# Lacing the two late layers: differential attention beside three products, output-projection chunks beside attention units

## The chip, the cores and the metric

One core of one Trainium2 chip runs the whole program; the other cores are idle. The metric is the device time of one execution in microseconds (us). Three executions of the kernel before gave 1477.77, 1477.8 and 1483.44 us, median 1477.8. Engines are named PE (TensorE), DVE (VectorE), ACT (ScalarE), POOL (GpSimd) and SP (SyncE, which issues the weight loads). Each engine runs its own instructions strictly in program order and waits on semaphores for the others.

## What is computed

A first block (gated linear attention, block attention, attention to a memory, then a mixture of 32 experts) gives `x`, 256 tokens by 1024 in float32. The second block, where the change lies, has two layers:

```
def second_block(x, c, ada_w, ada_b, ...):
    cond = jax.nn.silu(c)
    for l in range(2):
        mod = cond @ ada_w[l] + ada_b[l]                    # 1024 x 6144
        sh1, sc1, g1, sh2, sc2, g2 = split(mod, 6)
        h = rms_norm(x, norm_mix[l]) * (1 + sc1) + sh1
        y = even_mixer(h) if l == 0 else odd_mixer(h)
        x = x + g1 * (y @ w_out[l])
        h = rms_norm(x, norm_ffn[l]) * (1 + sc2) + sh2
        x = x + g2 * ((silu(h @ wg) * (h @ wu)) @ wd)       # hidden 2816

def even_mixer(h):      # aq, ak, av, bq, bk, bv, iq, ik, iw = columns of h @ w_in
    aq, ak = rms_norm per 64-wide head            # 4 heads x 2 maps
    ya = rms_norm(softmax(aq1 ak1') v - lam * softmax(aq2 ak2') v)
    score = sum over 8 heads of relu(iq ik') * iw;  sel = top 64 keys of each query
    yb = softmax over sel of rms_norm(bq) rms_norm(bk)'  times bv     # 8 heads
    return concat(ya, yb)

def odd_mixer(h):       # 16 query heads, 4 key heads, window of 128, a sink logit per head
```

## The kernel before

**Loads.** Weights come in loads of up to 2 MB on SP's DMA queue, in one fixed order, into a ring of `NR = 5` slots. `make_plan` writes that order out by hand. A load waits (`sp.wait_ge(*freed[before[k]])`) until the last user of what lay in its slot is done, and every later load stands behind that wait.

**Chunks.** A product (`ak`, `aq`, `av`, `kvi`, `tli`, `bq` in layer 0; `kvo`, `q0`, `q1` in layer 1), an output projection (`wo`) or a feed-forward matrix is worked in chunks of a 128-row strip. For each chunk ACT makes the rounded part (`W_c_r` or `X_c_r`), DVE the rest (`ring_r`), and PE multiplies in three terms: 12 matmuls of 512 columns, or 24 of 256. `Feed` has PE some chunks behind the two others (`lag`, 5 in the products).

**Modulation.** The 24 strips v0 to v23 of `cond @ ada_w` (`ada`) are spread between other work. A *run* needs a load of its own of 2 MB and is 8 matmuls on PE, `ps7<-ring,csr`; ACT copies the sum out; a *close*, 4 matmuls `ps7<-ones,acc`, spreads it, and DVE writes it to `modc`. All use bank 7, so the next run waits for DVE's `modc` of the strip before. The trace counts two passes for each f32 matmul: 16 records a run, 8 a close. `plan.rows` says at which chunk ("f"), norm ("n") or attention unit ("u") each stands.

**Attention.** `attend(n)` works units of a head and a query half in a pipeline of ticks: PE in each tick turns the weights of unit t-3, makes the two scores of unit t, multiplies the values of unit t-4; DVE takes maxima and makes weights, ACT exponentials. t2 (differential, 8 units), t3 (selected, 8) and t4 (sliding window, 16) are run one after another with nothing but modulation runs and side work (headnorms, turns, the indexer's selection) between them. Two units' scores are on different banks (`2 * (U % 2) + m`).

**Order.** Layer 0: `ak aq av kvi tli bq`, then t2 with the indexer beside it, t3, `wo1`, feed-forward. Layer 1: `kvo q0 q1`, t4, `wo2`, feed-forward. Only the first two chunks of `wo` are begun (split) inside the attention before them.

Of the kernel before, what the change touches and what calls it, by code (L numbers as in the profile page):

```python
# [76 lines left out]
class Feed:  # L77
# [36 lines left out]
def pipeline(n, *stages):  # L114
    for t in range(n + max(lag for lag, _ in stages)):
        for lag, stage in stages:
            if 0 <= t - lag < n:
                stage(t - lag)


class Plan:
# [51 lines left out]
    def ffn(self, l, turn_run, run):  # L173
# [63 lines left out]
def build(nc, A, out_ap, dbg):  # L237
    ctx = ExitStack()
    with ctx:
# [175 lines left out]
        beside = {first["wo", j] + c for j in range(3) for c in range(2)}  # L415
        buf, last_use, previous = [], {}, []
        for i in range(nch):
            if i == first["ak"]:
                last_use = {}
            b = min(range(3 if i in beside else 6), key=lambda z: (last_use.get(z, -1), z))  # L420
# [135 lines left out]
        bank = (0, 0, 1, 1, 2, 2, 3, 4)  # L556
        block_of = lambda f: ps[bank[f]][:, half(f) if f < 6 else slice(0, 256)]
# [14 lines left out]
        class Attn:  # L572
            total, values, outs, done = 0, [], 0, 0

            def __init__(self, X, hL, units):
# [3 lines left out]
                self.pv, self.fin, self.oh = [], [], []  # L579
                for unit in units:  # L580
# [207 lines left out]
        def scalar(act):  # L788
# [59 lines left out]
            def attend(n, beside, chunks=(), XF=None):  # L848
# [21 lines left out]
                def copies(u):  # L870
# [4 lines left out]
                    copy(at_n.pT[:, U % 2, 0:w], ps[4 + U % 2][:, 0:w], up=s_cp)  # L875
# [7 lines left out]
                pipeline(len(at_n.units), (4, copies), (5, fins), (1, weights), (0, scores), (4, ahead))  # L883

            def out_proj(j, tb, XF, attended):
                if j < 2:
                    act.wait_ge(s_gc, j + 1)
                    for c in range(4):
                        act.wait_ge(s_tp, tb + c + 1)
                        copy(hH[:, c, :], ps[4 + c][:, 0:256], scale=gc, up=s_tH)  # L890
                act.wait_ge(s_fin, attended)
                for c in range(2, 8):
                    begin(first["wo", j] + c, XF)
# [160 lines left out]

            def work_av():
# [27 lines left out]
            feed.product(first["av"], 4, ends("av", av, [4, 5], work_av()))  # L1083
            feed.product(first["kvi"], 4, ends("kvi", kvi, [0, 1], headnorm(heads(kvp[:, :, 0:64]), 1)))
            feed.product(first["tli"], 2, ends("tli", tli, [2, 3], steps(3)))
            feed.product(first["bq"], 4, ends("bq", bq, [4, 5], work_bq()))
            feed.drain()
            side.until(ev, "qk")
            attend(2, 2)
# [7 lines left out]
            attend(3, 2, [first["wo", 1], first["wo", 1] + 1], XFc)  # L1097
            side.end()
            ada(("o", 1))
            out_proj(1, 28, XFc, t3.end)  # L1100
# [65 lines left out]
        def vector(dve):  # L1166
# [88 lines left out]
            def attend(n, beside, chunks=(), XF=None):  # L1255
# [13 lines left out]
                def weights(u):  # L1269
# [7 lines left out]
                    for m in range(2):  # L1277
                        V(dve.tensor_tensor_reduce, at_n.pb[:, k, 257 * m:257 * m + nk], ps[2 * (U % 2) + m][:, 0:nk], unit.bias,
# [25 lines left out]
                pipeline(len(at_n.units), (1, weights), (2, norms), (5, fins), (0, scores), (4, ahead))  # L1304

            def out_proj(j, gain, hL, XF):
                if gain:
                    V(ts, gc, gain[0], gain[1], None, ALU.mult, up=s_gc)
                    for c in range(4):
                        dve.wait_ge(*C.next(s_tH))  # L1310
                        V(stt, out=hL[:, c, :], in0=ps[4 + c][:, 0:256], scalar=gc, in1=hH[:, c, :].bitcast(FP), op0=ALU.mult,
                          op1=ALU.subtract, up=s_tL)
                for c in range(2, 8):
                    begin(first["wo", j] + c, XF)
# [22 lines left out]
            def add_xT(gate, n, end):  # L1337
                for f in range(8):
                    if f == 7:
                        dve.wait_ge(s_use, end)  # L1340
                    elif f % 2 == 0:
                        dve.wait_ge(s_f, 4 * n + f // 2 + 1)
                    V(stt, out=xT[:, f, :], in0=block_of(f), scalar=gate[:, f:f + 1], in1=xT[:, f, :], op0=ALU.mult,
# [295 lines left out]

            def work_av():  # L1640
# [62 lines left out]
            feed.product(first["av"], 4, ends(work_av()))  # L1703
            feed.product(first["kvi"], 4, ends(work_kvi()))
            feed.product(first["tli"], 2, ends(work_tli()))
            feed.product(first["bq"], 4, ends(work_bq()))
            feed.drain()
            side.until(ev, "qk")
            attend(2, 2)
# [87 lines left out]
        def tensor(pe):  # L1797
# [108 lines left out]
            def features(i, j, last, xH, xL, XF):  # L1906
# [5 lines left out]
                for f in range(8):  # L1912
                    for n, row in both_last:
                        w, wl, wh = chunk(n, 1, XF)
                        for m, (x_, z) in enumerate(((xH, wh), (xL, wh), (xH, wl))):
                            t = mm(block_of(f), z[:, 0, 128 * f:128 * f + 128], x_[:, row, :],
                                   j == 0 and m == 0 and (f % 2 == 0 or f == 7), j == last and n == i and m == 2 and f % 2 == 1)
                        if f == 7:
                            t.then_inc(s_use, 1)
                    if j == last and f in (1, 3, 5, 6):  # L1920
                        t.then_inc(s_f, 1)
                if j == last:
                    for f in range(8):
                        free[bank[f]] = C.next(s_xd)
# [610 lines left out]
```

## Time and profile before

| | us |
|---|---|
| three runs, median | 1477.8 |
| profiled execution: time / span | 1480.7 / 1478.7 |
| PE busy | 1207.3 (82%) |
| DVE busy | 615.7 (42%) |
| ACT busy | 476.1 (32%) |
| DMA queue q1 | 367.26 MB, 64.7% of 16 engines |
| first block, until PE starts the second | about 697 |

Busy shares are of the whole span. In the profile PEclk is the TensorE clock granted, as a share of full speed; "PE idle, <- X" says whose result ended an idle stretch.

### The profile page before, as it was taken

How to read it: one execution, taken by the hardware profiler on the slowest of the kernel's cores; microseconds unless marked ns; L12 is line 12 of the kernel's file. 1: busy time of each engine (PE TensorE's matmuls, PEld its weight loads, DVE VectorE, ACT ScalarE, POOL GpSimd, SP SyncE). 2: the span in 40 equal slices, each digit the busy share in tenths (PEclk: the TensorE clock that was granted, in tenths of full speed). 3: DMA queues.
4: the chain of work that ended last, by engine and by line, in shares of the span. 5: the costliest groups of instructions: out<-in, count | busy, mean ns of one | idle time of the engine just before them, and what ended most of it. 6: DMA issues, size and time to landing. Idle time of an engine off the chain costs nothing.

```text
span 1478.7 us, 19441 instructions
## 1 busy us (share of the span) xinstructions
PE 1207.3 (82%) x7691; PEld 883.7 (60%) x7691; DVE 615.7 (42%) x1239; ACT 476.1 (32%) x769; POOL 7.6 (1%) x54
## 2 busy tenths in 40 slices
PE   5878886775676756847897888999999978999998
PEld 4655464442333323413675337899898734999986
DVE  3472643110010000101753576655535756565553
ACT  4561530100000000002532335554433447465441
POOL 1000000000000000000000000000000000000000
PEclk9897788888888877977897668899999988999999
DMA  8442347999999999999536431865536462665520
GB/s 292 172 152 76 115 173 320 428 430 429 430 430 428 430 430 428 430 425 403 197 129 228 171 114 58 253 207 201 195 145 226 171 253 90 203 196 174 203 109 29
DMA packets 121728, 368.67 MB, mean 249 GB/s; under 512 B 9842, under 2 KB 56093, under 8 KB 110878
## 3 DMA queue, kind: packets, MB, share of 16 engines
q1 hardware_dynamic: 120556, 367.26, 64.7%
q8 instruction: 64, 1.05, 0.3%
q10 hardware_dynamic: 1074, 0.08, 0.1%
q14 instruction: 34, 0.28, 0.1%
HBM read 366.28 MB, written 1.05 MB: 248 GB/s over the span
## 4 chain that ended last, share of the span: by engine, by line
PE 61%; DMA 21%; DVE 9%; ACT 5%; issue 3%; SPq 1%; DVEq 0%; ACTq 0%
PE ps L1810 58%; DMA more<-in_w_down_dram 7%; DMA more<-in_w_gate_dram 7%; DMA more<-in_w_up_dram 6%; PE ps L1814 3%; DVE st L32 2%; DVE ring_r L32 2%; DVE R_c L32 1%; SPq L664 1%; DVE R_a L32 1%; DVE X_c L32 1%; ACT X_c L32 1%; DVE sc L32 1%; ACT R_a L32 1%; ACT hn L32 1%
## 5 line engine op out<-in xcount | busy, mean ns | idle before, releaser
L1810 PE MATMUL ps<-hT_r,ring_r 128*128 128x256 f32 x864 | 245.5, 284 | 0.0
L1810 PE MATMUL ps<-ring,xg 128*32 128x512 f32 x640 | 140.4, 725 | 121.5 <-DMA more<-in_w_gate_dram 42.6
L1810 PEld LDWEIGHTS ps<-hT_r,ring_r 128*128 128x128 f32 x864 | 167.8, 194 | 0.0
L1810 PEld LDWEIGHTS ps<-ring,xg 128*32 128x32 f32 x640 | 35.2, 131 | 217.2 <-issue 217.2
L32 DVE TENSOR_TENSOR ring_r<-ring,W_c_r 128x1024 fp32r<-128x1024 f32 x94 | 115.2, 1226 | 97.5 <-ACT W_c_r L32 94.1
L1810 PE MATMUL ps<-R_c_r,W_c_r 128*128 128x256 f32 x608 | 153.1, 284 | 0.0
L32 DVE TENSOR_TENSOR ring_r<-ring,X_c_r 128x1024 fp32r<-128x1024 f32 x88 | 107.8, 1225 | 98.4 <-ACT X_c_r L32 95.7
L1810 PE MATMUL ps<-R_c_r,X_c_r 128*128 128x256 f32 x576 | 148.2, 285 | 0.0
L32 ACT ACTIVATE W_c_r<-ring 128x1024 fp32r<-128x1024 f32 x94 | 99.7, 1060 | 89.2 <-PE ps L1810 84.5
L32 ACT ACTIVATE X_c_r<-ring 128x1024 fp32r<-128x1024 f32 x88 | 93.3, 1061 | 90.3 <-PE ps L1810 85.4
L1810 PE MATMUL ps<-hT_r,W_c_r 128*128 128x256 f32 x416 | 119.0, 286 | 1.9 <-DVE R_c_r L32 1.8
L1810 PE MATMUL ps<-hT_r,X_c_r 128*128 128x256 f32 x416 | 119.0, 286 | 1.8 <-DVE R_c_r L32 1.8
L32 DVE TENSOR_TENSOR x<-x,ps 128x512 f32<-128x512 f32 x36 | 24.8, 688 | 228.9 <-PE ps L1810 228.6
L1810 PEld LDWEIGHTS ps<-R_c_r,W_c_r 128*128 128x128 f32 x608 | 109.2, 191 | 0.0
L1810 PEld LDWEIGHTS ps<-R_c_r,X_c_r 128*128 128x128 f32 x576 | 104.6, 192 | 1.7 <-issue 1.7
L1810 PE MATMUL ps<-ring_r,hT_r 128*128 128x512 f32 (+1 forms) x240 | 97.7, 407 | 0.0
L1810 PEld LDWEIGHTS ps<-hT_r,W_c_r 128*128 128x128 f32 x416 | 79.9, 192 | 2.7 <-DVE R_c_r L32 2.2
L1810 PEld LDWEIGHTS ps<-hT_r,X_c_r 128*128 128x128 f32 x416 | 79.9, 192 | 2.6 <-issue 2.5
L1810 PE MATMUL ps<-ring,csr 128*32 128x512 f32 x384 | 66.8, 830 | 13.0 <-DVE modc L32 12.5
L1810 PE MATMUL ps<-more,xg 128*32 128x512 f32 x384 | 72.6, 747 | 0.0
L1810 PE MATMUL ps<-sel,hn 128*128 128x128 f32 x256 | 63.1, 408 | 2.4 <-DVE sel L32 2.4
L1810 PEld LDWEIGHTS ps<-sel,hn 128*128 128x128 f32 x256 | 61.8, 336 | 3.2 <-DVE flag L32 2.5
(281 smaller groups left out, 1874.5 us busy)
## 6 DMA issues: line engine op xcount, KB each, us to landing
ring<-in_ada_w_dram SPq DMA_DIRECT2D x24, 2048.0 KB, 8.2
ring<-in_w_gate_dram SPq DMA_DIRECT2D x20, 2048.0 KB, 15.9
ring<-in_w_up_dram SPq DMA_DIRECT2D x20, 2048.0 KB, 20.7
ring<-in_w_down_dram SPq DMA_DIRECT2D x20, 2048.0 KB, 16.4
more<-in_w_up_dram SPq DMA_DIRECT2D x12, 2048.0 KB, 24.4
more<-in_w_gate_dram SPq DMA_DIRECT2D x12, 2048.0 KB, 23.1
more<-in_w_down_dram SPq DMA_DIRECT2D x12, 2048.0 KB, 23.6
ring<-in_ffn_gate_dram SPq DMA_DIRECT2D x22, 1024.0 KB, 5.6
```

What stands on the lines that cost most here:

```text
L32: op(*args, **kw).then_inc(sem, 1)
L664: sp.dma_start(dst, src).then_inc(s_w[slot[k]], 16)
L1810: return pe.matmul(out, lhsT, rhs, start=start, stop=stop, skip_group_check=True)
L1814: return pe.transpose(out, in_, ident[0:n, 0:n])
```

## The change

Three things, all in the second block.

1. `attend` now returns its ticks as a generator. `beside_first` steps t2's ticks between the chunks of `kvi`, `tli`, `bq`, with `lag` 2; these three products all write banks 4 and 5. Their ACT and DVE buffers are taken from 3 instead of 6 (`narrow`). Since t2 now starts before `kvi`'s second chunk, the turn of `aq` must be done by then, and PE, DVE and ACT run `side.until(ev, "qk")` there.
2. `beside` steps t3's and t4's ticks with a chunk of `wo1` or `wo2` every second tick (from tick 2, from tick 4); these sums are on banks 3, 4, 5, 7. For t3, modulated heads from t2 are turned in tick 5 (`mix_turned`).
3. To free banks, scores of t2, t3, t4 are on banks 0 and 1 for every unit, and turned weights on 2 (t2: 2 and 3). Bank 7 is needed for `wo`, so fewer modulation strips lie in the attentions, and more in the products and feed-forwards.

```diff
+def beside(g, units, feed, i0, start, hook):
+    n = 0
+    for t in range(units + 5):
+        next(g, None)
+        if t == start + 3:
+            feed.side.end()
+            hook()
+        if t >= start and (t - start) % 2 == 0:
+            if n < 8:
+                feed(i0 + n)
+                n += 1
+            else:
+                feed.one()
+    for k in range(n, 8):
+        feed(i0 + k)
+    feed.drain()
...
-    for name in ("aq", "av", "kvi"):
-        p.product(name, 4)
+    for name in ("aq", "av"):
+        k = p.load("w", name)
+        p.first[name] = len(p.chunks)
+        for q in range(4):
+            if q == 1:
+                p.ada(("f", len(p.chunks)))
+            if q == 3:
+                p.close(("f", len(p.chunks)))
+            p.feed(k, q)
+    p.product("kvi", 4)
     p.product("tli", 2)
-    p.ada(("f", len(p.chunks)))
     p.product("bq", 4)
-    p.close(("f", len(p.chunks) - 1))
     p.units(2, 8, (0, 2, 4, 6))
-    p.units(3, 8, (0, 2, 4, 6), 2, 1)
-    p.close(("o", 1))
+    p.units(3, 8, (0, 2), 0, 1)
     p.out_proj(1)
-    p.ffn(0, True, 6)
+    p.ffn(0, True, (6, 12))
...
     p.product("q0", 4)
-    p.product("q1", 4)
-    p.units(4, 16, (0, 2, 4, 6, 8, 10, 12), 8, 2)
-    p.close(("o", 2))
+    p.ada(("f", len(p.chunks)))
+    k = p.load("w", "q1")
+    p.first["q1"] = len(p.chunks)
+    for q in range(4):
+        if q == 2:
+            p.close(("f", len(p.chunks)))
+        if q == 3:
+            p.ada(("f", len(p.chunks)))
+        p.feed(k, q)
+    p.units(4, 16, (1, 3, 5), 1, 2)
     p.out_proj(2)
-    p.ffn(1, False, None)
+    p.ffn(1, False, (6, 12))
...
+        for t_ in (t2, t3, t4):
+            t_.score = lambda U, m: m
+        t2.turned = lambda U: 2 + U % 2
+        t3.turned = t4.turned = lambda U: 2
...
+        def beside_first(feed, g, ready):
+            feed.lag = 2
+            for i in range(first["kvi"], first["bq"] + 4):
+                feed(i)
+                if i == first["kvi"]:
+                    ready()
+                else:
+                    next(g)
+            feed.drain()
+            run(g)
```

**What moves, place 1.** PE between the second block's first modulation run (v4) and the first chunk of `ak` (`ps0<-W_c_r,hT_r`). Before:

```order
L1810 MATMUL ps7<-ring,csr 32x512 [waits s_w3,s_gather_out]
L1810 MATMUL ps7<-ring,csr 32x512 x7
L1810 MATMUL ps6<-ident,sc 128x128 [waits s_norm_rstd_spread]
L1810 MATMUL ps6<-ident,sc 128x128
L1810 MATMUL ps0<-W_c_r,hT_r 128x512 [waits s_lo,s_tL,s_moe_hid,s_moe_silu]
```

After:

```order
L1857 MATMUL ps7<-ring,csr 32x512 [waits s_w3,s_gather_out]
L1857 MATMUL ps7<-ring,csr 32x512 x7
L1857 MATMUL ps6<-ident,sc 128x128 [waits s_norm_rstd_spread]
L1857 MATMUL ps6<-ident,sc 128x128
L1857 MATMUL ps7<-ones,acc 128x1 [waits s_ada_copied]
L1857 MATMUL ps7<-ones,acc 128x1 x3
L1857 MATMUL ps7<-ring,csr 32x512 [waits s_w0,s_ada_col]
L1857 MATMUL ps7<-ring,csr 32x512 x7
L1857 MATMUL ps0<-W_c_r,hT_r 128x512 [waits s_lo,s_tL,s_moe_hid,s_moe_silu]
```

The close of v4 and the run of v5 now stand ahead of the first chunk. `s_w0` is v5's load; `s_ada_col` is DVE's write of `modc` for v4. On DVE that write stands here, after:

```order
L32 SCALAR_TENSOR_TENSOR R_c_r<-R_c,modc,hT_r 128x256 [waits s_tL,s_tH]
L32 TENSOR_TENSOR ring_r<-ring,X_c_r 128x1024 [waits s_tL,s_hi]
L32 TENSOR_TENSOR ring_r<-ring,X_c_r 128x1024 [waits s_lo,s_hi]
L32 TENSOR_TENSOR modc<-ps7,cols 128x4 [waits s_lo,s_ld1,s_ada_closed]
L32 TENSOR_TENSOR ring_r<-ring,W_c_r 128x1024 [waits s_ada_col,s_hi]
```

It is behind the last modulated rest (`R_c_r`) and two splits of later chunks.

**Place 2.** PE at the end of `ak` (`ps1`) and the start of `aq` (`ps2`). Before, one product follows the other:

```order
L1810 MATMUL ps1<-X_c_r,hT_r 128x512
L1810 MATMUL ps1<-X_c_r,R_c_r 128x512
L1810 MATMUL ps1<-ring_r,hT_r 128x512
L1810 MATMUL ps2<-X_c_r,hT_r 128x512 [waits s_lo,s_moe_y,s_scatter_added]
```

After, v6's run is between them:

```order
L1857 MATMUL ps1<-X_c_r,hT_r 128x512
L1857 MATMUL ps1<-X_c_r,R_c_r 128x512
L1857 MATMUL ps1<-ring_r,hT_r 128x512
L1857 MATMUL ps7<-ring,csr 32x512 [waits s_w2,s_ada_col]
L1857 MATMUL ps7<-ring,csr 32x512 x7
L1857 MATMUL ps2<-X_c_r,hT_r 128x512 [waits s_lo,s_moe_y,s_scatter_added]
```

Slot 2 (`s_w2`) held `ak`'s weights, so v6's load is issued only when the row above the run is done. The planner's table of slots gives the same for v7 (slot of `av`), v9 (slot of `kvi`), v10 (slot of `tli`) and v18 (slot of `kvo`).

**Place 3.** PE after the last chunk of `kvi`. Before, the close of v5 and `tli` (on `ps2`, `ps3`) follow:

```order
L1810 MATMUL ps1<-X_c_r,hT_r 128x512
L1810 MATMUL ps1<-X_c_r,R_c_r 128x512
L1810 MATMUL ps1<-ring_r,hT_r 128x512
L1810 MATMUL ps7<-ones,acc 128x1 [waits s_ada_copied]
L1810 MATMUL ps7<-ones,acc 128x1 x3
L1810 MATMUL ps2<-X_c_r,hT_r 128x256 [waits s_lo,s_evacuated]
```

After, a tick of t2 and v9's run are between `kvi` (`ps5`) and `tli` (`ps4`):

```order
L1857 MATMUL ps5<-W_c_r,hT_r 128x512
L1857 MATMUL ps5<-W_c_r,R_c_r 128x512
L1857 MATMUL ps5<-ring_r,hT_r 128x512
L1861 MATMUL ps3<-ident,X_c 128x128 [waits s_attn_normed,s_evacuated]
L1861 MATMUL ps3<-ident,X_c 128x128
L1857 MATMUL ps0<-R_c 128x128 [waits s_attn_max]
L1857 MATMUL ps1<-R_c 128x128 [waits s_attn_max]
L1857 MATMUL ps7<-ring,csr 32x512 [waits s_w3,s_ada_col]
L1857 MATMUL ps7<-ring,csr 32x512 x7
L1857 MATMUL ps6<-R_c,X_c 128x128 [waits s_attn_copied,s_head_copied]
L1857 MATMUL ps4<-W_c_r,hT_r 128x256 [waits s_lo,s_evacuated]
```

What moved in: turned weights on `ps3`, the two scores on `ps0` and `ps1`, a run that waits for slot 3 (`kvi`'s own, just freed), and a value product on `ps6`.

## Rows read from the trace of the kernel before

**Rows 1.** Windows: stretch, length, busy PE, PEld, DVE, ACT, POOL, clock, DMA share, GB/s

```profile
700.00:792.00 92.00, 83.43 (x387) 64.70 (x386) 51.59 (x101) 35.44 (x47) 0.00 (x0) 0.89 0.53 186
792.00:858.00 66.00, 48.20 (x208) 26.26 (x208) 36.44 (x137) 21.44 (x57) 0.69 (x2) 0.66 0.45 160
858.00:900.00 42.00, 32.61 (x200) 16.04 (x200) 30.88 (x104) 19.41 (x54) 0.00 (x0) 0.70 0.30 101
925.00:1145.00 220.00, 212.86 (x1732) 204.22 (x1731) 117.77 (x155) 98.80 (x126) 0.00 (x0) 0.94 0.61 206
1184.00:1275.00 91.00, 77.77 (x563) 50.26 (x562) 53.77 (x158) 50.21 (x115) 0.00 (x0) 0.87 0.47 162
```

**Rows 2.** PE's waits, 740 to 950: us in total, times, longest

```profile
PE ps L1814 <- DVE R_c L32: 7.7, 5, 5.0
PE ps L1810 <- DVE modc L32: 6.3, 5, 2.2
```

**Rows 3.** PE's timeline, 709 to 715: start, length, instruction

```profile
709.71 0.47 PE L1810 MATMUL ps<-W_c_r,hT_r 128*128 128x512 f32 x1 [1.77 <-DVE R_c_r L32]
...
710.53 0.63 PE L1810 MATMUL ps<-W_c_r,hT_r 128*128 128x512 f32 x1
710.95 0.63 PE L1810 MATMUL ps<-W_c_r,R_c_r 128*128 128x512 f32 x1
...
714.60 0.39 PE L1810 MATMUL ps<-ring_r,hT_r 128*128 128x512 f32 x1
714.83 0.40 PE L1810 MATMUL ps<-W_c_r,hT_r 128*128 128x512 f32 x1
```

**Rows 4.** DVE's timeline, 720 to 724

```profile
720.69 2.56 DVE L32 TENSOR_TENSOR ring_r<-ring,X_c_r 128x1024 fp32r<-128x1024 f32 x2 [1.24 <-ACT X_c_r L32]
```

**Rows 5.** PE's timeline, 755 to 760

```profile
755.48 1.05 PE L1810 MATMUL ps<-ones,acc 128*128 128x1 f32 x8 [1.66 <-DVE R_c L32]
757.11 2.61 PE L1810 MATMUL ps<-ring,csr 128*32 128x512 f32 x16 [0.57 <-DVE modc L32]
```

**Rows 6.** DMA issues of the page: KB each, median us from issue to landing

```profile
ring<-in_ada_w_dram SPq DMA_DIRECT2D x24, 2048.0 KB, 8.2
```

**Rows 7.** Groups by form, 792 to 858: count, busy, mean ns, idle before

```profile
L1810 PE MATMUL ps<-R_c,X_c 128*128 128x128 f32 x24 | 6.9, 418 | 4.6 <-DVE hn L32 4.6
L1814 PE MATMUL ps<-ident,X_c 128*128 128x128 f32 x12 | 3.5, 358 | 0.0
L32 DVE CUSTOM_DVE_ANT_0 X_c<-ps,negd 128x256 f32<-128x256 f32 x8 | 3.4, 424 | 0.8 <-DVE modc L32 0.7
L32 DVE COPY hn<-ps 128x128 f32<-128x128 f32 x8 | 2.3, 291 | 4.6 <-PE ps L1810 4.2
```

**Rows 8.** PE's timeline, first instruction of `wo1` and the one behind it

```profile
902.09 0.55 PE L1810 MATMUL ps<-hT_r,W_c_r 128*128 128x256 f32 x1
...
926.09 4.28 PE L1810 MATMUL ps<-ones,sc 128*128 128x1 f32 x32
```

**Rows 9.** PE's timeline, 1066 to 1075, in the feed-forward of layer 0

```profile
1066.71 0.95 PE L1810 MATMUL ps<-ones,acc 128*128 128x1 f32 x8
1071.26 3.64 PE L1810 MATMUL ps<-ring,csr 128*32 128x512 f32 x16 [3.60 <-DVE modc L32]
```

**Rows 10.** PE's timeline in t4 and `wo2`: units 2, 4, 6, first and last of `wo2`

```profile
1200.38 0.80 PE L1810 MATMUL ps<-R_c 64*128 64x128 f32 x4
...
1207.53 0.49 PE L1810 MATMUL ps<-R_c 64*128 64x128 f32 x4
1207.95 1.92 PE L1810 MATMUL ps<-ring,csr 128*32 128x512 f32 x16
...
1213.33 0.49 PE L1810 MATMUL ps<-R_c 64*128 64x128 f32 x4
...
1251.70 0.58 PE L1810 MATMUL ps<-hT_r,W_c_r 128*128 128x256 f32 x1 [1.84 <-DVE R_c_r L32]
...
1276.60 3.63 PE L1810 MATMUL ps<-ones,sc 128*128 128x1 f32 x32
```

More of the change, by code:

```diff
@@ L411, in build @@
         nch = plan.end
-        beside = {first["wo", j] + c for j in range(3) for c in range(2)}
+        narrow = {first["wo", j] + c for j in range(3) for c in range(8 if j else 2)}
+        narrow |= set(range(first["kvi"], first["bq"] + 4))
         buf, last_use, previous = [], {}, []
@@ L881, in fins, with mix_turned @@
                         copy(hH[:, unit.dst, unit.out], ps[6][:, unit.out], up=s_oh)
[L883 to L893, printed above, removed]
+                return ticks(len(at_n.units), (4, copies), (5, fins), (1, weights), (0, scores), (4, ahead))
+            def mix_turned(j, tb):
+                act.wait_ge(s_gc, j + 1)
+                for c in range(4):
+                    act.wait_ge(s_tp, tb + c + 1)
+                    copy(hH[:, c, :], ps[mixed[j][c]][:, 0:256], scale=gc, up=s_tH)
             def modulated(l, which, n, ready, hooks={}):
@@ L1082, in scalar @@
             feed.product(first["aq"], 4, ends("aq", aq, [2, 3], work_aq()))
[L1083 to L1089, printed above, removed]
+            feed.product(first["av"], 4, ends("av", av, [4, 5], steps(2)))
+            feed.then[first["kvi"] + 3] = ends("kvi", kvi, [4, 5], headnorm(heads(kvp[:, :, 0:64]), 1))
+            feed.then[first["tli"] + 1] = ends("tli", tli, [4, 5], steps(3))
+            feed.then[first["bq"] + 3] = ends("bq", bq, [4, 5], work_bq())
+            beside_first(feed, attend(2, 2), lambda: side.until(ev, "qk"))
             def work_sub():
@@ L1302, in fins, with mix_turned @@
                           up=s_fin)
[L1304 to L1314, printed above, removed]
+                return ticks(len(at_n.units), (1, weights), (2, norms), (5, fins), (0, scores), (4, ahead))
+            def mix_turned(j, gain, hL):
+                V(ts, gc, gain[0], gain[1], None, ALU.mult, up=s_gc)
+                for c in range(4):
+                    dve.wait_ge(*C.next(s_tH))
+                    V(stt, out=hL[:, c, :], in0=ps[mixed[j][c]][:, 0:256], scalar=gc, in1=hH[:, c, :].bitcast(FP), op0=ALU.mult,
+                      op1=ALU.subtract, up=s_tL)
             def add_x(gate, n, end):
@@ L1702, in vector @@
             feed.product(first["aq"], 4, ends(work_aq()))
[L1703 to L1709, printed above, removed]
+            feed.product(first["av"], 4, ends(steps(2)))
+            feed.then[first["kvi"] + 3] = ends(work_kvi())
+            feed.then[first["tli"] + 1] = ends(work_tli())
+            feed.then[first["bq"] + 3] = ends(work_bq())
+            beside_first(feed, attend(2, 2), lambda: side.until(ev, "qk"))
             def work_sub():
@@ L2154, in tensor @@
             pe.wait_ge(s_fin, t1.end)
-            out_proj(0, hL_ma, XF, 16)
+            mix_turned(0)
+            feed = out_proj(0, hL_ma, XF, 16)
+            for c in range(8):
+                feed(first["wo", 0] + c)
+            feed.drain()
             pe.wait_ge(s_hn0, 3)
```

152 lines of the change are left out of this document (77 added, 75 removed).

## Prediction

> **What bounds the kernel now.** I read first the windows by stage, then PE's waits, then PE's timeline stage by stage. In the second block PE sets the end. In the feed-forward, 925 to 1145, it is busy 212.86 of 220 us; in the products before t2, 83.43 of 92 (8.6 us idle). Only the attentions have room: 48.20 of 66 us with t2 and the indexer, 32.61 of 42 with t3, 77.77 of 91 with t4 and `wo2` [rows 1]. There DVE (36.44 and 30.88 us) is no bound by itself either; units wait for each other in a chain of PE, DVE and ACT, and PE is granted only 0.66 and 0.70 of its clock. In PE's list of waits from 740 to 950 the longest entries name DVE: headnorm results (`R_c`, 7.7 us, one of 5.0) and `modc`, 6.3 [rows 2]. There is no row for a DMA: every load lands before its user. So the change can win the idle time of the attentions, about 18 + 9 + 13 us and the slow clock in them, if it adds no waits of its own elsewhere. I find that it does, by its placing of the modulation strips.
>
> **Layer 0, until `bq` is done.** In before that is T = 791.9, the start of t2. Five terms.
>
> (a) v5's run now stands ahead of `ak`. Before, the first chunk begins at 709.71 [rows 3]. Now PE must wait there for v4's `modc`, which DVE writes behind all modulated rests and two splits; these two end at 720.69 + 2.56 = 723.25 [rows 4], and what they need doesn't come from `ak`. Write and run: 723.25 + 0.2 + 3.64 (a run after a wait, rows 9) = 727.1. The first chunk starts at 727.1 instead of 709.71: **+17.4**. ACT and DVE have their next chunks split by then, but only six buffers are there, and PE is the bound behind it, so nothing of it is won back.
>
> (b) More strips. Before, this stretch held two closes and a run, 1.05 + 2.61 + 0.95 = 4.6 [rows 5, 9]. Now the runs of v6 to v10 and six closes. Four of the runs follow a wait for a load and take 3.64, one 1.92 [rows 9, 10]; closes 1.05: 14.6 + 1.9 + 6.3 = 22.8. **+18.2.**
>
> (c) t2's own PE work now lies in it: all value products are 6.9 us and turns 3.5 [rows 7], scores some 0.6 for each of 8 units [rows 10]: 15.2 for all in the slow clock. With most units in and a faster clock beside chunks I take **+10** (8 to 15).
>
> (d) PE's waits. A load takes 8.2 us from issue to landing [rows 6]. v6's load needs `ak`'s slot, and v6's run is the very next thing on PE: 8.1. v7 after `av`: only a unit's scores between, 7.5. v9 after `kvi`: a turn and scores, 7.2. v10 after `tli`: a headturn besides and what DVE is late, 5.0. Sum 27.8. The turn of `aq` must be ready by `kvi`'s second chunk, where before all of `av` lay between; the nearest row is the wait of 5.0 for a headnorm [rows 2], and two splits of 1.28 [rows 4] stand before it on DVE: 7.4. Together 35.2, less the 8.6 that were there [rows 1]: **+27**. Bounds: from 15 (if two of the waits fall into one of DVE's) to 36.
>
> (e) Behind a long wait, a chunk's first nine matmuls come 0.42 us apart instead of 0.23 [rows 3], 1.7 us a time; three times: **+5**. This is the TensorE clock at its lower level (1.2 of 2.4 GHz): after PE's idle 3.60 us the run took 3.64, in the flow 1.92 [rows 9, 10]. The Trainium skill (TensorE: Matmul & The Clock Gate, HAM oscillation — how this bites in real kernels) describes just this: bursts of matmuls parted by waits for a DMA start in the slow clock each time. By that rule the sum stays as it is, and without it it would be 5 us less and (b) 7 less; the trace agrees.
>
> Sum 17.4 + 18.2 + 10 + 27 + 5 = **+78**.
>
> **Layer 0, from there to the end of `wo1`.** Before, 791.9 to 926.1 [rows 8], 134.2 us. Now t2's work on DVE is gone from it: the wide maxima 3.4 and the copies of `hn` 2.3 [rows 7], and with the narrow maxima, weights, norms and small steps about 18 of the 36.44 [rows 1]. The indexer's chain (relu, weighted sums, eight rounds of maxima, then t3) stays and has to wait for `bq`'s and `tli`'s results as before. Of `wo1`, 24.0 us for 8 chunks [rows 8], half is in t3 now (chunk c ≥ 4 waits for the last unit): −12. Together −30, with a little single banking **−29** (−18 to −37). Where it could be less: a chunk's two splits cost DVE 1.28 and ACT alike inside ticks that the chain fills.
>
> **Feed-forward 0**: one run and close more, no stall: 1.92 + 0.95 = **+2.9**.
>
> **Layer 1.** In `q1` the close of v16 and run of v17 meet the stall seen at 1066.71 (0.95, then 3.60 idle and a run of 3.64 [rows 9]): +8.2. Then close v17 1.05, wait for v18's load (slot of `kvo`, issued long before) at most 1.5, run 1.92: **+12.7** (5 to 15; in before a like stall lies in unit 0, and I leave units 0 and 1 as they were, since v18's close and v19's run will stand there). From unit 2 to the end of `wo2`: before 1276.60 − 1200.38 = 76.2 [rows 10]. Pairs of units with a run and a close take 5.8 (1207.53 to 1213.33 [rows 10]), so without these 2.8. After: three pairs with strips, 16.5; then a pair and a chunk of 2.9 are 5.7, and with both scores on the same two banks for each unit, so that a unit's scores wait for the maxima of the one before, I take 6.4, four times: 25.6; the tail 10.6; what is left of `wo2` 7.5. Sum 60, −16; against it stands that each pair could as well wait for DVE (splits and weights), 1 us each. **−14** (−20 to −6). Feed-forward 1 gets v22 and v23, the wide gates: 1.92 + 2.25 each, **+8.3**. Layer 1: **+7**.
>
> **Sum.** 78 − 29 + 2.9 + 7 = +59. The profiled execution took 1480.7, so 1539.6; it was 2.9 above the median of the three, so **1537**.
>
> **The rivals.**
>
> 1. *Loads and restarts cost little* (chance 0.12). PE's waits in (d) replace others, since DVE and ACT are behind there too and catch up. For it: DVE's and ACT's splits of the next chunk do run on during a wait. Against: before has only 8.6 us to be replaced [rows 1]. Time: without 27 + 5, and 7 less in (b): 1498.
>
> 2. *Laced ticks are slower than I make them* (0.12). With three chunk buffers and lag 2, each tick of t2 beside a chunk goes through DVE's queue: split, maxima, weights; with one pair of score banks unit t+1 can't start before the maxima of t. Every tick of 10, 6 and 8 would be 1 to 2 us longer, at 24 ticks +25 to +40: 1562 to 1575. Against: DVE is busy only 36.44 of 66 us [rows 1].
>
> 3. *It wins, because PE's idle time is filled* (faster, 0.04). Mechanism: strips' loads land behind other work, v5's run costs only itself, and attention lies under chunks. Then (a), (d) and (e) fall away, 17.4 + 27 + 5 + 7: 1481, and layer 0's second half and t4 at their best bounds (−8, −6) give 1467. It decides at PE's wait before v6: if PE isn't seen idle for a DMA there, this or rival 1 holds; if the first chunk of `ak` begins near 711 as well, this. Beside it: the Trainium skill (Perfetto Trace Analysis, Optimization Strategy) says that interleaving stretches with different busiest engines may help. This case's stretches are such [rows 1]; the rule speaks for the change, and says nothing of loads that come in a ring.
>
> **How the numbers follow.** My own case has 0.70; its range, from the bounds of (c), (d), the second half, t4 and q-phase taken together as roots (2 to 5, 12, 11, 8, 8: about ±18), is 1519 to 1556. Rival 1 gives 1498 and rival 2 1562 to 1575; with 0.12 each, the range for 8 in 10 takes in part of both: 1506 to 1563. 0.02 are left for no change by other sums. About 0.5%, 7 us, is what a measurement can tell: faster 0.04, same 0.03, slower 0.93.
>
> **What the profile after would show.** PE idle about 12 us before the first `ak` chunk, with `modc` as its releaser; PE idle for `ring<-in_ada_w_dram` about 8, 7.5, 7 and 5 us behind `ak`, `av`, `kvi` and `tli`; runs of 3.6 us behind these; the stretch from the end of `bq` to `wo1`'s end some 105 us; t4 from unit 2 to the end of `wo2` about 62; the feed-forwards as before but for three strips. I would be wrong most likely in the ticks beside chunks, where no row of before shows a product and an attention sharing DVE.

## The result

The changed kernel takes 1564.0 us (median of 4 runs, 1563.0 to 1566.7), the kernel before 1479.6 beside it: ratio 1.057, 95% interval 1.0542 to 1.0598. It is slower by about 84 us, as forecast in sign, but 1 us above my range and 27 above my value. The profiled span is 1562.6 us against 1478.7.

The windows of the changed kernel, by the same stretches as [rows 1] (length, busy PE, PEld, DVE, ACT, POOL, clock, DMA share, GB/s):

```profile
702.00:794.00 92.00, 58.05 (x258) 41.13 (x257) 36.83 (x74) 25.08 (x34) 0.00 (x0) 0.76 0.36 129
794.00:873.00 79.00, 57.82 (x304) 38.49 (x304) 29.92 (x96) 24.82 (x56) 0.00 (x0) 0.82 0.24 87
873.00:985.00 112.00, 74.61 (x410) 52.81 (x409) 67.89 (x190) 38.86 (x83) 0.69 (x2) 0.70 0.37 132
985.00:1203.00 218.00, 211.33 (x1743) 201.97 (x1742) 117.42 (x155) 99.14 (x128) 0.00 (x0) 0.98 0.61 208
1256.00:1350.00 94.00, 73.02 (x492) 51.62 (x492) 54.19 (x157) 47.55 (x110) 0.00 (x0) 0.82 0.28 92
```

In the first 92 us of the second block PE is now busy 58.05 us, where it was busy 83.43 [rows 1]. The feed-forward is as it was. Where the time went, by PE's start times (us) at the same places of the two profiles:

| place on PE | before | after | added here | my term |
|---|---|---|---|---|
| start of the second block | 696.93 | 698.73 | 1.8 | 0 |
| first chunk of `ak` | 709.71 | 729.09 | 17.6 | 17.4 |
| `bq` done | 791.9 | 872.7 | 61.4 | 60 |
| `wo1` done | 926.09 | 984.69 | −22.2 | −29 |
| first chunk of `kvo` | 1144.76 | 1203.41 | 0.1 | 2.9 |
| t4, unit 0 | 1183.73 | 1255.90 | 13.5 | 12.7 |
| t4, unit 2 | 1200.38 | 1271.26 | −1.3 | 0 |
| `wo2` done | 1276.60 | 1349.64 | 2.2 | −14 |
| first chunk of feed-forward 1 | 1285.31 | 1360.93 | 2.6 | 0 |
| end of the span | 1478.7 | 1562.6 | 8.3 | 8.3 |

PE's timeline of the changed kernel, the runs and closes of layer 0's products (start, length, instruction, idle before):

```profile
721.58 1.84 PE L1857 MATMUL ps<-ones,acc 128*128 128x1 f32 x8 [11.70 <-ACT acc L32]
725.52 3.64 PE L1857 MATMUL ps<-ring,csr 128*32 128x512 f32 x16 [2.10 <-DVE modc L32]
...
749.48 3.64 PE L1857 MATMUL ps<-ring,csr 128*32 128x512 f32 x16 [7.94 <-DMA ring<-in_ada_w_dram]
...
781.67 1.97 PE L1861 MATMUL ps<-ident,R_c 128*128 128x128 f32 x8 [6.98 <-DVE R_c L32]
...
796.28 3.64 PE L1857 MATMUL ps<-ring,csr 128*32 128x512 f32 x16 [6.14 <-DMA ring<-in_ada_w_dram]
...
827.41 3.64 PE L1857 MATMUL ps<-ring,csr 128*32 128x512 f32 x16 [7.56 <-DMA ring<-in_ada_w_dram]
...
849.20 3.51 PE L1857 MATMUL ps<-ring,csr 128*32 128x512 f32 x16 [4.77 <-DMA ring<-in_ada_w_dram]
```

All waits that I had named are there: for the loads of v6, v7, v9 and v10, 26.4 us together (27.8 forecast), and 6.98 for the headnorm of `aq` (7.4). The wait before v5's run isn't quite the one that I had named. Its larger part is that of the close, for ACT's copy of v4's sum (11.70), and only 2.10 for `modc`. ACT's timeline shows why the copy is late:

```profile
720.24 0.51 ACT L32 ACTIVATE hT_r<-R_c,modc 128x256 fp32r<-128x256 f32 x1 [0.60 <-DVE R_c L32]
720.84 0.60 ACT L32 ACTIVATE acc<-ps 128x512 f32<-128x512 f32 x1
```

The copy (`acc<-ps`) stands behind the last of ACT's modulated copies (`hT_r`), as DVE's `modc` stands behind the rests.

In t4 of the changed kernel PE's list of waits (total, times, longest) reads, 1256 to 1350:

```profile
PE ps L1857 <- DVE s L32: 8.0, 4, 5.9
PE ps L1857 <- DVE R_c_r L32: 5.5, 6, 1.8
PE ps L1861 <- ACT X_c L32: 3.5, 4, 1.3
```

`DVE s` is the read of the maxima: PE waits for it before it writes the next unit's scores to banks 0 and 1. It has no row in t4 before, but 5.9 of its 8.0 us lie ahead of unit 2, and there they stand in the place of a wait of before. DVE has the headnorm of `q1` to do first in both kernels, and PE is held up by whatever DVE does behind it. In the changed kernel, then in before:

```profile
1263.27 1.61 PE L1857 MATMUL ps<-R_c 64*128 64x256 f32 x4 [5.90 <-DVE s L32]
```

```profile
1190.33 3.64 PE L1810 MATMUL ps<-ring,csr 128*32 128x512 f32 x16 [5.12 <-DVE modc L32]
```

The timeline's marks of units 2 and 8 in the changed kernel:

```profile
1271.26 0.49 PE L1857 MATMUL ps<-R_c 64*128 64x128 f32 x4
...
1276.42 3.23 PE L1857 MATMUL ps<-ring,csr 128*32 128x512 f32 x16
...
1300.05 0.80 PE L1857 MATMUL ps<-R_c 64*128 64x128 f32 x4
```

Units 2 to 8 take 28.8 us; before, units 2 to 6 took 13.0 [rows 10] and 2 to 8 took 18.8. I had 16.5. From unit 8 on, with chunks being multiplied, the pairs take 8.7, 6.9 and 7.2, where I had 6.4.

The windows of just these units, before and after, split the 10 us:

```profile
1200.38:1219.14 18.76, 18.71 (x140) 9.44 (x139) 10.99 (x43) 10.23 (x30) 0.00 (x0) 0.87 0.74 273
```

```profile
1271.26:1300.05 28.79, 22.81 (x124) 12.52 (x123) 14.30 (x49) 12.23 (x33) 0.00 (x0) 0.70 0.19 61
```

PE is idle for 6.0 us, before for 0.05: in its list of waits 3.5 for ACT's copy of the turned weights, 2.1 for the maxima, 0.4 for a headnorm. The other 4.1 us are PE's busy time, at a granted clock of 0.70 instead of 0.87.

### The profile page after: what moved, and what is told of

It reads as the page before. It is cut to its first block, busy times and chain, and to the rows that moved or that the text cites. A ratio compares the mean times of both kernels' runs of the same rounds, so it can differ in the third digit from the quotient of the medians.

```text
span 1562.6 us, 19448 instructions
## 1 busy us (share of the span) xinstructions
PE 1212.3 (78%) x7691; PEld 887.2 (57%) x7691; DVE 615.7 (39%) x1239; ACT 476.0 (30%) x769; POOL 7.6 (0%) x54
## 4 chain that ended last, share of the span: by engine, by line
PE 55%; DMA 23%; DVE 13%; ACT 5%; issue 3%; SPq 1%; DVEq 0%; ACTq 0%; POOL 0%; POOLq 0%
PE ps L1857 53%; DMA more<-in_w_down_dram 7%; DMA more<-in_w_gate_dram 7%; DMA more<-in_w_up_dram 6%; DVE ring_r L32 3%; DMA ring<-in_ada_w_dram 3%; PE ps L1861 2%; DVE st L32 2%; DVE R_c L32 2%; DVE X_c L32 1%; SPq L728 1%; DVE R_c_r L32 1%; ACT W_c_r L32 1%; DVE R_a L32 1%; ACT X_c L32 1%
## 5 line engine op out<-in xcount | busy, mean ns | idle before, releaser
L32 DVE TENSOR_TENSOR ring_r<-ring,W_c_r 128x1024 fp32r<-128x1024 f32 x104 | 127.4, 1225 | 160.8 <-ACT W_c_r L32 157.4
L1857 PE MATMUL ps<-R_c_r,W_c_r 128*128 128x256 f32 x656 | 167.0, 285 | 0.0
L32 ACT ACTIVATE W_c_r<-ring 128x1024 fp32r<-128x1024 f32 x104 | 110.1, 1059 | 95.1 <-PE ps L1857 90.0
L1857 PE MATMUL ps<-hT_r,W_c_r 128*128 128x256 f32 x464 | 133.3, 287 | 1.0 <-DVE R_c_r L32 1.0
L1857 PE MATMUL ps<-R_c_r,X_c_r 128*128 128x256 f32 x528 | 133.1, 283 | 0.0
L32 DVE TENSOR_TENSOR ring_r<-ring,X_c_r 128x1024 fp32r<-128x1024 f32 x78 | 95.6, 1226 | 87.9 <-ACT X_c_r L32 85.4
L1857 PE MATMUL ps<-hT_r,X_c_r 128*128 128x256 f32 x368 | 104.8, 285 | 2.2 <-DVE R_c_r L32 1.8
L32 ACT ACTIVATE X_c_r<-ring 128x1024 fp32r<-128x1024 f32 x78 | 82.7, 1060 | 75.7 <-PE ps L1857 71.6
L1857 PE MATMUL ps<-R_c 64*128 64x128 f32 (+1 forms) x160 | 43.2, 475 | 31.8 <-DVE s L32 21.7
L1857 PE MATMUL ps<-W_c_r,R_c_r 128*128 128x512 f32 (+1 forms) x192 | 67.4, 392 | 0.0
```

The lines of the kernel that those rows point to most:

```text
L32: op(*args, **kw).then_inc(sem, 1)
L1857: return pe.matmul(out, lhsT, rhs, start=start, stop=stop, skip_group_check=True)
```

## The experiments

All times are medians, beside the kernel before on the same chip; "ratio" is to it, with its 95% interval.

**Halves of the change.** e1 sets only the banks, e2 and e3 lace one layer, e4 has only the strips' new places.

```diff
 # e1: the kernel before, and
+        for t_ in (t2, t3, t4):
+            t_.score = lambda U, m: m
+        t2.turned = lambda U: 2 + U % 2
+        t3.turned = t4.turned = lambda U: 2
 # e2: the changed kernel, layer 1 as before; e3: layer 0 as before, as in
-            beside(attend(4, 1), 16, Feed(...), first["wo", 2], 4, lambda: None)
+            run(attend(4, 1, [first["wo", 2], first["wo", 2] + 1], XFc))
 # e4: make_plan of the changed kernel, all products and attentions as before
```

> The kernel before, in which only the banks of the three late attentions change as in the changed kernel: scores of every unit on banks 0 and 1, turned weights on 2 (t2: 2 and 3). No lacing, strips where they were. Theory A (the attentions beside chunks cost more than I forecast because PE may not start a unit's scores until DVE has taken the maxima of the unit before): +15 to +30 us, and PE's list of waits shows the read maxima (DVE s) before the scores of t2, t3 and t4. Theory B (it is the chunks' own work in the ticks, on DVE and ACT, that lengthens them): within 5 us of before, no such waits.

> The changed kernel with layer 1 as before (strips, banks and order of t4 and the output projection). Both theories: the share of layer 0 in the loss, by the two profiles +57 us (1536). If the two layers hang together by their loads, the two halves would not add up to +84.

> The changed kernel with layer 0 as before. By the two profiles layer 1 loses 13.5 in the products, 1 to 3 in t4 with wo2, 2.6 in the norm behind it, 8.3 in the feed-forward: +25 us (1505). My prediction had +7 for it.

> The kernel before with the modulation strips at the places of the changed kernel; no lacing, banks as before. Theory of the placing (the prediction's terms a, part of b and d, and the products and feed-forward of layer 1): the bubble before the first ak chunk 17.4, v6's wait for its load 8 and its slow run, layer 1's products 13.5, the feed-forward 8.3, less the four strips no longer in t4 and two no longer in t3 (about -16): +30 to +40 us. Rival (strips are work that must lie somewhere, PE work is the same, placing is neutral): within 10 us of before.

Measured, with before at 1482.0: e1 1495.8 (ratio 1.013, 1.007 to 1.018), e2 1537.5 (1.040, 1.035 to 1.044), e3 1502.8 (1.015, 1.012 to 1.019), e4 1511.6 (1.021, 1.018 to 1.025). e2 and e3 are within 3 us of what I expected (1536 and 1505). The two layers' losses, 55.5 and 20.8, add up to 76 of the 84: most of the loss is the sum of two separate ones. e4 shows that 30 us are lost with no lacing at all, at the lower edge of the theory of the placing (30 to 40); its rival (within 10) falls. Its list of PE's waits, 700 to 1000, has the two that I had put on the strips' places:

```profile
PE ps L1875 <- ACT acc L32: 12.8, 4, 11.7
PE ps L1875 <- DMA ring<-in_ada_w_dram: 8.0, 1, 8.0
```

e1 came out at the lower end of theory A, but not by its mechanism in t4. The maxima have no row there; PE's waits in e1, 1187 to 1268, are for ACT's copy of the turned weights:

```profile
PE ps L1820 <- ACT X_c L32: 8.6, 10, 1.1
PE ps L1816 <- DVE modc L32: 5.1, 1, 5.1
```

**Which bank costs.** e5 is e1 without the lines on `turned`.

> The kernel before with only the scores of t2, t3, t4 on banks 0 and 1; turned weights keep their two banks 4 and 5. In t4 of e1 PE waited ten times about 1.06 us for ACT's copy of the turned weights and never for the maxima. Theory A1 (the single bank of the turned weights is the price): this run is within 4 us of before, 10 to 12 less than e1. Theory A2 (the scores' banks are the price): as e1, +12 to +16.

1485.7 beside 1479.3, ratio 1.0036 (1.0017 to 1.0055); the profiled spans are 1483.7 and 1493.7 (e1). So of e1's price some 5 us belong to the scores and about 10 to the single bank of the turned weights; e1's interval is wide (10 to 27 us above before), so the 10 are rough. A1 holds for most of it, and the scores are not free.

By stage the picture is another one. Up to the end of `wo1` e5 takes 229.7 us (before 229.2), e1 235.6: there the turned weights' bank costs. Yet both have the same waits for the maxima in t2 and t3 (6.4 us, four times, the longest 3.0), so in e5 these waits for the maxima only took the place of others. In t4, units 2 to 14 take 38.4 us before, 45.6 in e5 and 48.7 in e1, and most of that is already in e5, with the scores' banks alone. In units 2 to 8 its list of waits has just one, of 0.7 us; PE is busy longer, at a clock of 0.71:

```profile
1198.03:1222.96 24.93, 24.08 (x140) 11.11 (x139) 11.11 (x44) 10.28 (x30) 0.00 (x0) 0.71 0.61 216
```

**Are the strips' places the loss of layer 0?** e6 moves v5's run alone, e7 all strips that met a wait.

```diff
 # e6
-            if q == 1:
-                p.ada(("f", len(p.chunks)))
-            if q == 3:
-                p.close(("f", len(p.chunks)))
+            if (name, q) in (("aq", 1), ("av", 0), ("av", 3)):
+                p.close(("f", len(p.chunks)))
+            if (name, q) in (("aq", 3), ("av", 1)):
+                p.ada(("f", len(p.chunks)))
 # e7
+    p.product("aq", 4)
+    p.close(("f", len(p.chunks)))
+    p.product("av", 4)
+    p.ada(("f", len(p.chunks)))       # v5; closed at kvi+2
...
-    p.units(2, 8, (0, 2, 4, 6))
+    p.units(2, 8, (2, 6))
     p.units(3, 8, (0, 2), 0, 1)
     p.out_proj(1)
-    p.ffn(0, True, (6, 12))
+    p.ffn(0, True, (2, 6, 10, 14, 18))
...
-    p.units(4, 16, (1, 3, 5), 1, 2)
+    p.units(4, 16, (0, 2, 4, 6), 0, 2)
```

> The changed kernel with v4's close kept at aq+1 and v5's run moved two chunks on, so that PE has two chunks of ak to do while DVE writes modc. If the 17.4 us before the first ak chunk come from that wait alone: 1564 - 17 = 1547, first ak chunk near 711. If the wait only hides one that follows (ak's chunks, the loads behind it): less than 8 us gained.

> The changed kernel, laced as it is, with the strips placed so that no run follows the release of its slot within 8 us and every close stands two chunks ahead of the next run: v4's close at av+0, v5 at kvi+0, v6 and v7 in t2, v11 to v15 in the feed-forward of layer 0, v16's close at q0+2, v17 at q1+0, v18 to v21 in t4 at even units. Theory of the placing: without the 17, the four waits for loads of 26.4, their slow clock of about 12 and the stall of 4 to 6 in layer 1: 1564 - 60 = about 1505, still above before. Rival (PE's waits for loads cover waits for DVE that would show instead): 1530 or more. Third (lacing pays once the strips are right): under 1478.

e6: 1563.8, no gain. I had expected 17. PE still waits at v4's close, in e6's timeline:

```profile
721.97 1.83 PE L1857 MATMUL ps<-ones,acc 128*128 128x1 f32 x8 [11.69 <-ACT acc L32]
```

Only the wait for `modc` went, and v5's run now lies among the chunks. The first chunk of `ak` starts 24.2 us after the block, where it started 30.4 after it in the changed kernel; from there to the end of `wo1` e6 takes 261.0 instead of 255.6, so nearly all of it is lost again. That was the second of the two outcomes that I had named (less than 8). The close is what must move. In e7 it stands at `av`'s first chunk, and the first chunk of `ak` starts at 712.21, 12.6 us after the start of the block (before: 12.8).

e7: 1541.3, ratio 1.040 (1.037 to 1.043). The number is in the rival's range (1530 or more), but mostly not by the rival's mechanism. From the start of the block to the end of `wo1` e7 takes 240.9 us, the changed kernel 286.0, before 229.2: the places were worth 45 us in layer 0 (55 forecast). Three strips fewer run there than in the changed kernel, some 9 of the 45 at 2.9 a strip. The feed-forward took back 21.5: it has the three strips, and with five strips among the 22 chunks of the down product, the ring is short again (PE's waits, 1060 to 1180):

```profile
PE ps L1862 <- DMA ring<-in_ada_w_dram: 13.3, 3, 4.6
```

And with the best places that I found, layer 0 laced is still 12 us longer than not laced, though four strips fewer run in it than before. Seven profiles of kernels with nothing changed up to there have 225.4 to 229.2 for this stretch, so the 12 us are clear of the spread.

**Which lacing pays?** e10 laces t3 with `wo1` alone, e11 t2 with the products alone; both space the strips.

```diff
 # e10: beside(attend(3, 2), ...) kept, t2 and t4 run as before
+    p.units(3, 8, (0, 2), 0, 1)
+    p.ffn(0, True, (6, 12, 18))
 # e11: beside_first(feed, attend(2, 2), ...) kept, t3 and t4 run as before
+    p.units(2, 8, (2, 6))
+    p.ffn(0, True, (5, 11, 17))
```

> The kernel before with t3 and wo1 laced alone, single banks in t3 alone, two strips moved from t3 to the feed-forward of layer 0, the close of the strip before them ahead of its run. By terms: half of wo1 hidden -12, two strips +5.8, single banks +3 to +5: 1476 to 1481, equal to before. If laced chunks don't fit into DVE's and ACT's share of the ticks: +5 or more.

> The kernel before with t2 and the three products laced alone, strips spaced as in e7 (v5 before kvi, v6 and v7 in t2, three in the feed-forward), single scores in t2 alone. e7's layer 0 came out 12 us longer than before with t2 and t3 laced. If the lacing of t2 is the losing one: +10 to +15; if it gains (its idle time of 18 us filled): -5 or better.

e10: 1482.3, ratio 1.0018 (0.9999 to 1.0037), no change that can be told. `wo1` is done 229.3 us after the start of the block, as before (229.2), with two strips fewer in it. Half of its products are hidden; PE's waits from 858 to 930, in which before has no row for the maxima, show what stands against the gain:

```profile
PE ps L1858 <- DVE s L32: 9.5, 4, 6.3
PE ps L1862 <- ACT X_c L32: 2.1, 2, 1.5
```

A large part of these is DVE's own queue. In the changed kernel, whose longest wait of this kind is 6.92, DVE takes a unit's maxima at 919.12, then does rounds of the indexer's selection from 920.59 on with a chunk's split among them, and takes the next unit's maxima at 930.62 (PE's line, then DVE's):

```profile
930.98 1.13 PE L1857 MATMUL ps<-R_c 64*128 64x128 f32 x4 [6.92 <-DVE s L32]
```

```profile
920.59 0.43 DVE L32 MAX8 st<-R_c 128x8 f32<-128x256 f32 x1
...
930.62 0.29 DVE L32 CUSTOM_DVE_ANT_0 X_c<-ps,R_c 128x128 f32<-128x128 f32 x1 [0.17 <-DVE R_c L32]
```

e11: 1491.6, ratio 1.0083 (1.0050 to 1.0116): t2's lacing is the losing one, by 9.6 us up to the end of `wo1`, where two strips fewer run than before; 10 to 15 were expected of that. Its longest wait is the 7.0 for the headnorm of `aq`, which `av` no longer covers, and 5.6 for copies of `hn`.

**Why are t4's units 2 to 8 slow?** e9 begins `wo2`'s chunks in tick 8, so that no split is in these units; e13 and e14 have the strips at units 2, 4, 6 instead of 1, 3, 5, chunks from tick 8 and from tick 4. All lace layer 1 alone.

```diff
-            beside(attend(4, 1), 16, Feed(...), first["wo", 2], 4, lambda: None)
+            beside(attend(4, 1), 16, Feed(...), first["wo", 2], 8, lambda: None)  # e9, e13
-    p.units(4, 16, (1, 3, 5), 1, 2)
+    p.units(4, 16, (2, 4, 6), 2, 2)                                               # e13, e14
```

> e3 (layer 1 laced alone) with wo2's first chunk begun in tick 8 instead of tick 4. Open: why t4's units 2 to 8 take 28.8 us in the changed kernel, 24 in e1 with the same single banks, 18.8 before. Theory C (ACT's and DVE's splits of the first chunks stand ahead of the exponentials and maxima in ticks 4 to 8): units 2 to 8 in about 24, two chunks fewer hidden (+6), total within 3 of e3. Theory D (the order of strips, runs at odd units): still 28 to 29, total e3 + 6.

> e9 with v19 to v21 run at t4's units 2, 4, 6 instead of 1, 3, 5. Theory D (strips at odd units lie between the wide scores and the turns and keep the pair long): units 2 to 8 in about 24 as in e1, clock 0.85, total e9 - 4. Theory E (the clock stays low because PE comes out of the wait at unit 1 with too little to do, wherever the strips are): 27 to 29 as e9.

> e3 with the same even strips, chunks begun from tick 4. If the splits cost nothing at even units either: as e13 with two chunks more hidden, e3 - 4. If ACT's and DVE's splits stand ahead of the turned copy there (e7: waits of 2.24 for ACT's copy, units 2 to 8 in 35): e3 + 5.

| run | strips | chunks begun | units 2 to 8, us | clock | time, us | ratio, interval |
|---|---|---|---|---|---|---|
| before | even | not laced | 18.8 | 0.87 | | |
| e4, banks as before | odd | not laced | 18.5 | 0.82 | | |
| e1 | even | not laced | 23.4 | 0.85 | 1495.8 | 1.013, 1.007 to 1.018 |
| e5, scores' banks alone | even | not laced | 24.9 | 0.71 | 1485.7 | 1.004, 1.002 to 1.006 |
| e13 | even | tick 8 | 25.2 | 0.77 | 1501.1 | 1.015, 1.010 to 1.021 |
| e9 | odd | tick 8 | 27.9 | 0.56 | 1505.4 | 1.018, 1.015 to 1.021 |
| e3 | odd | tick 4 | 31.0 | 0.61 | 1502.8 | 1.015, 1.012 to 1.019 |
| e14 | even | tick 4 | 35.4 | 0.64 | 1507.7 | 1.021, 1.016 to 1.026 |

How far can such a stretch be trusted? Seven profiles in which units 2 to 8 are as before (before, e2, e8, e10, e11, e12, e15) have 17.9 to 18.9 for it. With t4 laced as in the changed kernel there are three: 28.8, 28.8 (e6) and 31.0 (e3).

Windows of units 2 to 8, in the order e1, e13, e9, e14, one line of each kernel:

```profile
1203.61:1226.97 23.36, 20.55 (x140) 10.39 (x139) 11.10 (x44) 10.39 (x31) 0.00 (x0) 0.85 0.68 248
```

```profile
1209.76:1234.96 25.20, 22.48 (x140) 11.50 (x139) 11.73 (x47) 10.71 (x32) 0.00 (x0) 0.77 0.27 84
```

```profile
1208.40:1236.35 27.95, 25.67 (x123) 14.00 (x123) 12.11 (x48) 10.10 (x31) 0.00 (x0) 0.56 0.18 60
```

```profile
1205.96:1241.38 35.42, 28.57 (x139) 14.54 (x138) 14.02 (x48) 12.81 (x34) 0.00 (x0) 0.64 0.19 60
```

Theory C falls with e9 by the stretch (27.9, not 24), though the total is within 3 us of e3, as it said. At odd units the splits cost 0.9 to 3.1 us, no more than the spread of the laced stretch. D holds in part by e13: 25.2 and a clock of 0.77, where it said about 24 and 0.85; the two totals, 4 us apart, can't be told from each other. And odd units cost nothing where the banks are as before (e4). At even units the splits do cost: 10 us in the stretch (e14 against e13; e7, with strips and chunks placed alike, has 35.3), and e14's total is 5 above e3's, as expected, with intervals that overlap. ACT's timeline of e14 shows the mechanism, a chunk's split between the strip's copy and the copy of the turned weights, for which PE waits 2.24:

```profile
1218.53 0.60 ACT L32 ACTIVATE acc<-ps 128x512 f32<-128x512 f32 x1 [3.31 <-PE ps L1867]
1219.24 1.06 ACT L32 ACTIVATE W_c_r<-ring 128x1024 fp32r<-128x1024 f32 x1
1220.41 0.60 ACT L32 ACTIVATE X_c<-ps 128x512 f32<-128x512 f32 x1
```

So for the 10 us between before and the changed kernel (28.8) in these units: the single banks alone give 4.6 (e1) to 6.2 (e5, the scores' alone); strips at odd units 2.7 more (e9 against e13); lacing and splits the rest. The parts don't simply add, since the clock differs from row to row of the table.

**A version that beats both.** Two closes of the kernel before waited on nothing but their place. e8 moves them; e12 and e15 try a step more.

```diff
 # e8, in ffn, and ahead of q1
+                if 4 * u + q == 2:
+                    self.close(("f", len(self.chunks)))
...
+    p.close(("f", len(p.chunks)))
     p.product("q1", 4)
 # e12: e8, and v17's run at the third chunk of q1; t4's strips at units 2 to 12
 # e15: e8, and v4's close ahead of kvi
```

> The kernel before with two closes moved ahead of the run that waits for them: v14's from chunk 6 to chunk 2 of the down product, v16's from t4's first unit to the first chunk of q1. The stalls of 3.60 and 5.12 us on modc and the slow clock behind them (1.7 each) should go: -6 to -12 us. Rival: at t4's start DVE is late anyway (headnorm of q1), so only the first is gained, -4 to -5.

> e8 with v17's run in q1 as well, so that PE has no strip between t4's units 0 and 1, where it waits for DVE's modc before a headturn on bank 7. One strip more in a full stretch +2.9, the wait of 4.0 gone: e8 -1 us, and at best -4.

> e8 with v4's close at kvi's first chunk instead of together with v5's run. PE waited 0.57 for modc there and ran v5 in 2.61 instead of 1.92: at best e8 - 1.5, too little to be told from e8; above e8 by 2 or more if the close now waits for ACT's copy.

e8: 1472.1 beside 1479.3, ratio 0.9929 (0.9904 to 0.9955), faster by 7 us, at the near end of what I expected (6 to 12). The run that followed an idle stretch of 3.60 and took 3.64 [rows 9] is now

```profile
1068.39 1.92 PE L1813 MATMUL ps<-ring,csr 128*32 128x512 f32 x16
```

At t4's start the wait became smaller but didn't go: 4.02 for `modc` before a headturn on bank 7. e12 shows what is behind it. Without that strip PE waits at the same place

```profile
1187.11 1.11 PE L1822 MATMUL ps<-ident,R_c 128*128 128x128 f32 x4 [7.12 <-DVE R_c L32]
```

for the headnorm of `q1`: units 0 to 2 take 13.2 in both, and e12 is at 1484.3 (ratio 1.0041, 1.0020 to 1.0061), without a gain. Its loss against e8 is in two places: 4.3 us more in the products ahead of t4, where the strip now lies, and 5.4 idle on PE at the end of `wo2`. There ACT has waited for a load of the feed-forward, and DVE's splits of it stand ahead of the update of `x` that the norm needs:

```profile
1264.80 3.41 ACT L32 ACTIVATE X_c_r<-ring 128x1024 fp32r<-128x1024 f32 x3 [12.90 <-DMA ring<-in_ffn_up_dram]
```

e15: 1472.6, ratio 0.9960 (0.9939 to 0.9981), not to be told from e8.

## Why the prediction was right, and where it was wrong

**The sign and layer 0's first part** were right, and mostly by their mechanism. (a) forecast 17.4, measured 17.6; the step named DVE's `modc` as the wait, the rows show ACT's copy ahead of it (11.7) and `modc` (2.1), and e6 shows that this matters: with the wait that I had named taken away, 6 us were gained ahead of `ak` and lost again behind it. (b) to (e) forecast 60, measured 61.4, in part by luck. The waits for loads are in their places and at their size. But PE's waits in this stretch are 41.2 us instead of 8.6, so (d) is 33 where I had 27, while (e) didn't show: of the 240 matmuls of 512 columns in it, 21 last longer than 0.5 us, before 29. The two misses about cancel.

**The rule beside rival 3** (Trainium skill, Perfetto Trace Analysis, Optimization Strategy) speaks of stretches whose busiest engine changes. I wrote that this case's stretches are such, and that was a wrong reading: in [rows 1] PE is the busiest engine in every stretch (48.20 against 36.44 for DVE with t2, 32.61 against 30.88 with t3). So the rule's condition isn't met, and the runs don't decide on it; interleaving t2 cost 9.6 us (e11), interleaving t3 gained nothing (e10).

**The rule on the slow clock** (Trainium skill, TensorE: Matmul & The Clock Gate, HAM oscillation — how this bites in real kernels) is borne out for the runs: the four in layer 0 behind a wait for a DMA of 4.77 to 7.94 us took 3.5 to 3.64, the run in e8 without a wait 1.92. One in layer 1, behind a DMA wait of 1.66, took 1.92 as well. It isn't borne out for (e)'s chunks.

**The step that failed is the term for t4 with `wo2`**: "After: three pairs with strips, 16.5; then a pair and a chunk ... I take 6.4", −14 in all, measured +2.2. Unit 2 to the end of `wo2` took 78.4 us for my sum of 60. Of these 18, 12.3 are in units 2 to 8, 28.8 instead of 16.5; 3.6 in the three pairs behind them (22.8 for 19.2); the rest in the tail. I had left units 2 to 8 as before, less a bit, because no chunk is multiplied in them. But their banks, the splits of the first chunks on ACT and DVE and the strips' places are new there. The trace shows 6.0 us of waits, for the copy of the turned weights and for the maxima, and 4.1 of longer busy time at the lower clock. e1 and e5 show that single banks alone, with nothing laced, already cost 4.6 and 6.2 in these units, and 10 and 7 in units 2 to 14. That is as much as hiding `wo2` won: from unit 14 to its end 26.8 us instead of 37.8. Why the clock is lower there stays open.

Another 2.6 came from the norm behind `wo2`, for which I had no term: PE stood idle for 1.94 ahead of its 32 small matmuls, and these took longer.

**A smaller miss**: the second half of layer 0 gave back 22.2 instead of 29. PE's list of waits, 873 to 985, has

```profile
PE ps L1857 <- DVE s L32: 12.5, 4, 6.9
PE ps L1857 <- ACT R_c L32: 7.4, 8, 4.0
```

where the wait for maxima (12.5) has no row in before; "a little single banking" stood for 1. How much of the 12.5 is a loss isn't shown: e5 has 6.4 of such waits in t2 and t3 and ends `wo1` 0.5 later than before, and the longest, 6.92, is spent behind DVE's selection and a split. With the turned weights' bank single as well, e1 lost 6.5 up to the end of `wo1`, which is the size of this miss. The feed-forward cost 0.1 instead of 2.9; the stall before its first run was a bit shorter (3.25, then a run of 3.05) and its granted clock higher (0.98, before 0.94).

**Rival 2** ("laced ticks are slower than I make them"), with 1562 to 1575, holds the measured time, and so does a good part of its mechanism: in t3 the maxima behind DVE's queue, in t4 the ticks of units 2 to 8. It had no word on the copy of the turned weights or on the clock. I had given it 0.12, and let the range end one microsecond into it. (The roots of my own case's bounds give ±20, not ±18; the measured time lies outside of both.) Rival 1 fell: e7 got 45 us back in layer 0 when the waits were taken away, so they covered little; some 9 of the 45 are strips that moved away. Rival 3 fell: even spaced, t2's lacing loses 10 (e11) and t3's gains nothing (e10).

## What to carry to other kernels

Before two stages are laced, write down which buffer each gives up for it, and price every one, small ones too: a single bank that two engines pass back and forth makes each unit wait for the one before, and the single banks alone cost in t4 (7 to 10 us) about what the hidden products gained (11). A load whose slot is freed by the instruction ahead of its user costs nearly its full latency (7.94 us of 8.2 here); look at the ring's table of slots, not at the bandwidth. Close what the next step waits for some chunks early: it costs nothing and gained more here (7 us) than all the lacing.

## What the runs showed of the hardware that I had not expected

The granted clock in t4's units 2 to 8 ranged from 0.56 (e9) to 0.87 (before) for nearly the same instructions. In e9 PE was busy for 25.67 of 27.95 us, before for 18.71 of 18.76: at the lower level the same matmuls are busy for longer. e9's waits from unit 2 on are none above 1.4 us, and the level came back only with the first chunk of 24 matmuls. In e5 one wait of 0.7 is all that the list of waits has in these units, and the clock was 0.71 all the same. Which waits decide it stays open.
